# Query and key items of an indexer interleaved on one core, with value weights and first value tile moved into the stage

## What is computed

```python
xn = rms_norm(h, g)
cb, cc, ch, q, k, v, qi, ki, iw = split_projection(xn @ w_in, pos, q_g, k_g)
# qi: 8 indexer queries of 64 per token, rotated; ki: one indexer key of 64, rotated; iw: 8 head weights
dots = jnp.einsum('bthd,bsd->bths', qi, ki)
scores = jnp.einsum('bths,bth->bts', jax.nn.relu(dots), iw) * IDX_SCALE
# top-k of the scores chooses the keys of the attention; v are its values
```

## Time and profile before

| | before |
|---|---|
| median of 3 runs | 1865.98 us (1863.97 to 1866.81) |
| profiled execution | 1866.83 us, span 1865.0 us |
| TensorE busy, mean granted clock | 1721.9 us (92%), 0.955 |
| VectorE busy | 1116.0 us (60%) |
| ScalarE busy | 812.2 us (44%) |
| GpSimd busy | 732.3 us (39%) |

### The profile page before, as it was taken

One profiled execution on the slowest core, in us unless ns is written; L12 is line 12 of the kernel. 1 busy time (PEld: TensorE's weight loads), 2 busy tenths in 40 slices (PEclk: granted clock), 3 DMA queues, 4 the chain that ended last, 5 costly groups with the idle time before them and its releaser, 6 DMA issues.

```text
span 1865.0 us, 33809 instructions
## 1 busy us (share of the span) xinstructions
PE 1721.9 (92%) x13803; PEld 1193.3 (64%) x13803; DVE 1116.0 (60%) x1901; ACT 812.2 (44%) x1475; POOL 732.3 (39%) x705
## 2 busy tenths in 40 slices
PE   6899999996876889999979998999999999999998
PEld 3554444443444655444568644788888888898998
DVE  4965665787797865356645227878878887400000
ACT  5456487753643864332356315544434434210100
POOL 3131266887530110320032516666666666401200
PEclk9899999997986999999977999999999999999999
DMA  7031212122424110301244212112121122221211
GB/s 227 6 105 41 56 35 64 50 74 82 141 94 139 53 47 1 110 1 35 72 155 130 86 40 91 46 46 69 46 64 52 47 69 86 97 94 40 94 35 29
DMA packets 136548, 132.75 MB, mean 71 GB/s; under 512 B 15358, under 2 KB 109630, under 8 KB 136356
## 3 DMA queue, kind: packets, MB, share of 16 engines
q1 hardware_dynamic: 123850, 118.79, 20.5%
q10 hardware_dynamic: 12544, 11.80, 2.0%
HBM read 114.58 MB, written 15.98 MB: 70 GB/s over the span
## 4 chain that ended last, share of the span: by engine, by line
PE 72%; DVE 12%; ACT 6%; issue 3%; POOL 3%; DMA 2%; SPq 0%; ACTq 0%; DVEq 0%; POOLq 0%
PE PS L1533 22%; PE PS L937 5%; PE PS L938 5%; PE PS L939 5%; PE PS L1590 5%; PE PS L1591 5%; PE PS L1592 5%; ACT arena L1606 2%; ACT arena L1665 2%; PE PS L1088 2%; PE PS L1090 2%; PE PS L1089 2%; PE PS L1235 2%; PE PS L1247 1%; POOL arena L2917 1%
## 5 line engine op out<-in xcount | busy, mean ns | idle before, releaser
L1533 PE MATMUL PS<-arena 128*128 128x272 f16 (+1 forms) x3696 | 430.5, 280 | 5.9 <-issue 5.9
L1533 PEld LDWEIGHTS PS<-arena 128*128 128x128 f16 (+1 forms) x3696 | 362.6, 98 | 73.8 <-issue 6.1
L1606 ACT ACTIVATE arena<-PS 128x512 f16<-128x512 f32 (+13 forms) x380 | 190.1, 530 | 234.8 <-PE PS L939 85.2
L368 POOL TENSOR_TENSOR arena<-arena 128x512 bf16<-128x512 f32 (+2 forms) x152 | 166.6, 1132 | 241.8 <-ACT arena L359 241.5
L1606 ACT ACTIVATE arena<-arena 128x512 f16<-128x512 f32 (+5 forms) x214 | 136.1, 657 | 235.5 <-PE PS L1533 116.0
L937 PE MATMUL PS<-arena 128*128 128x512 f16 (+3 forms) x648 | 231.2, 366 | 2.3 <-DVE arena L2557 1.4
L938 PE MATMUL PS<-arena 128*128 128x512 f16 (+3 forms) x648 | 230.8, 365 | 0.0
L939 PE MATMUL PS<-arena 128*128 128x512 bf16 (+3 forms) x648 | 230.4, 364 | 0.0
L1590 PE MATMUL PS<-arena 128*128 128x256 f16 (+1 forms) x792 | 216.0, 273 | 1.4 <-POOL arena L915 1.0
L1592 PE MATMUL PS<-arena 128*128 128x256 bf16 (+1 forms) x792 | 215.9, 273 | 0.0
L1591 PE MATMUL PS<-arena 128*128 128x256 f16 (+1 forms) x792 | 215.9, 273 | 0.0
(11 more groups left out here) (350 smaller groups left out, 3712.5 us busy)
## 6 DMA issues: line engine op xcount, KB each, us to landing
arena<-w_gu SPq DMA_DIRECT2D x44, 512.0 KB, 4.8
arena<-w_down SPq DMA_DIRECT2D x8, 1408.0 KB, 7.7
arena<-w_in SPq DMA_DIRECT2D x8, 1024.0 KB, 5.5
arena<-w_kv_mem SPq DMA_DIRECT2D x8, 1024.0 KB, 5.3
arena<-cache_mem_k SPq DMA_DIRECT2D x32, 256.0 KB, 3.4
arena<-cache_mem_v ACTq DMA_DIRECT2D x28, 256.0 KB, 4.1
arena<-w_in SPq DMA_DIRECT2D x24, 256.0 KB, 3.9
arena<-x_prompt SPq DMA_DIRECT2D x9, 512.0 KB, 6.4
```

The lines of the kernel that those rows point to most:

```text
L368: x = e.tensor_tensor(w_lo[self.slot(n)][:, 4 * half + k, 0:width], wst[half][:, k, 0:width], w_hi[self.slot(n)][:, 4 * half + k, 0:width] ...
L1533: mm = e.matmul(PS[:, product_bank(f, i) + c, 0:TC], w[:, i, k], s[i][:, q, c, :], start=first, stop=last)
L1606: e.activation(out, in_, ACT.Copy, **kw).then_inc(sem(name), 1)
```

## The change

The items come in turns, query 0, then query j and key j - 1 for j = 1 to 8, then key 8, and all three loops run over items instead of steps. Slots of chunks are counted anew: the key weights get room of their own in the region `XM`, and the value weights take the slot that they leave. So the split of the value weights waits for nothing, and ScalarE does it in items 5 and 8, GpSimd in eight pieces behind the rotations of items 6 to 13. The first value tile (eight steps) is done by TensorE behind the projection of the last item and the transpose of query 8; the other 64 steps are spread over the 48 dots. SyncE stores the first seven keys before it loads three constants of the selection. Cut to its core:

```diff
-                if n >= 2:
-                    name, count = self.used(n - 2)
-                    e.wait_ge(sem(name), upto(name, count))
-                for half in range(2):
+                before = self.used(n - 2) if n >= 2 else None
+                if before:
+                    e.wait_ge(sem(before[0]), upto(*before))
+                for half in halves:
...
-                    lambda n: ("s2_mm", NT * (n + 1)) if n < 2 else ("v_mm", NT) if n == 2 else
-                    ("s4_mm", NT * (n - 2)) if n < 7 else ("s2_mm", NT * (n - 4)))
+                    lambda n: None if n == 0 else ("s2_mm", NI1) if n == 1 else ("v_mm", NT) if n == 2 else
+                    ("s4_mm", NT * (n - 2)) if n < 7 else ("s2_mm", NT * (n - 4)), odd=2,
+                    own={1: (view("XM", 0, [KT, D_IN - KIB], F16), view("XM", 2048, [KT, D_IN - KIB], BF16))})
...
-        ITEMS = [(c, j) for c in (A_QI, A_KI, A_Q, A_K) for j in range(NT)]
+        ITEMS = [(A_QI, 0)] + [it for j in range(1, NT) for it in ((A_QI, j), (A_KI, j - 1))] + [(A_KI, NT - 1)]
+        ITEMS += [(c, j) for c in (A_Q, A_K) for j in range(NT)]
...
         def values_upto(m):
-            return VSTEPS * max(0, m + 1) // ND
+            return KT + (VSTEPS - KT) * (m + 1) // ND if m >= -1 else 0
...
             A.load(e, 2)
+            store_roped(A_KI, range(NB - 1))
             e.wait_ge(sem("n1_lo"), NT)
...
-            store_roped(A_KI)
+            store_roped(A_KI, range(NB - 1, NT))
...
+            N1.pe_turn(e, 0, lambda j: h[0:rows(j), j, :])
+            for L in range(NI1 + 2):
+                if L < NI1:
+                    c, j = ITEMS[L]
+                    if c == A_QI:
+                        if j + 1 < NT:
+                            N1.pe_turn(e, j + 1, lambda j: h[0:rows(j), j, :])
+                        e.wait_ge(sem("n1_lo"), j + 1)
+                    if L >= 2:
+                        e.wait_ge(sem("s2_raw"), L - 1)
+                    project_item(L)
+                if L >= 2:
+                    turn_item(L - 2)
+                if L == NI1 - 1:
+                    e.wait_ge(sem("n1_lo"), NT)
+                    for k in range(KT):
+                        value_step(0, k)
...
+            N1.act_root(e, 1)
+            N1.act_hi(e, 0)
+            for L in range(NI1 + 2):
+                if L < NI1:
                     c, j = ITEMS[L]
+                    if c == A_QI and j + 2 < NT:
+                        N1.act_root(e, j + 2)
+                    if c == A_QI and j + 1 < NT:
+                        N1.act_hi(e, j + 1)
                     n, w = rows(j), A.chunks[c][1]
                     e.wait_ge(sem("s2_mm"), L + 1)
                     if L >= 3:
                         e.wait_ge(sem("s2_roped"), L - 2)
                     copy(raws[0][0:n, L % 3, 0:w], PS[0:n, L % 2, 0:w], "s2_raw")
-                    if j == 0:
-                        A.split_hi(e, c + 1)
-                if step >= 4:
-                    item_hi(step - 4)
+                    if L == 0:
+                        A.split_hi(e, A_KI)
+                    if L in (5, 8):
+                        A.split_hi(e, A_V, [int(L == 8)])
+                if L >= 2:
+                    item_hi(L - 2)
...
+            for j in range(3):
+                N1.dve_norm(e, j, lambda j: h[0:rows(j), j, :])
+                if j >= 1:
+                    N1.dve_lo(e, j - 1)
+            e.wait_ge(sem("turns_ld"), 32)
+            for L in range(NI1 + 2):
+                if L < NI1:
+                    c, j = ITEMS[L]
+                    if c == A_QI and j + 3 < NT:
+                        N1.dve_norm(e, j + 3, lambda j: h[0:rows(j), j, :])
+                    if c == A_QI and j + 2 < NT:
+                        N1.dve_lo(e, j + 2)
+                    project_item(L)
+                if L >= 2:
+                    item_lo(L - 2)
...
-            for n in range(3):
-                A.split_lo(e, n)
+            A.split_lo(e, A_QI)
+            A.split_lo(e, A_KI)
+            for half in range(2):
+                e.wait_ge(sem("wa_hi"), 2 * A_V + half + 1)
+                for k in range(4):
+                    e.wait_ge(sem("s2_roped"), 7 + 4 * half + k)
+                    x = e.tensor_tensor(A.low(A_V)[:, 4 * half + k, :], wst[half][:, k, :],
+                                        A.high(A_V)[:, 4 * half + k, :], ALU.subtract)
+                x.then_inc(sem("wa_lo"), 1)
```

More of the change, by code:

```diff
@@ L346, in load, with split_hi @@
                         c += w
-            def split_hi(self, e, n):
+            def split_hi(self, e, n, halves=(0, 1)):
                 if n >= len(self.chunks):
@@ L366, in split_lo @@
                     for k in range(4):
-                        x = e.tensor_tensor(w_lo[self.slot(n)][:, 4 * half + k, 0:width], wst[half][:, k, 0:width],
-                                            w_hi[self.slot(n)][:, 4 * half + k, 0:width], ALU.subtract)
+                        x = e.tensor_tensor(self.low(n)[:, 4 * half + k, :], wst[half][:, k, 0:width],
+                                            self.high(n)[:, 4 * half + k, :], ALU.subtract)
                     x.then_inc(self.s("lo"), 1)
@@ L694, in _, with store_roped @@
             const(pts[:, :], io["page_table"].rearrange("a b -> (a b)")[None, :])
-            def store_roped(c):
+            def store_roped(c, js=range(NT)):
                 for k in STORED:
-                    if ITEMS[k][0] == c:
+                    if ITEMS[k][0] == c and ITEMS[k][1] in js:
                         j = ITEMS[k][1]
@@ L994, in project_item, with value_step @@
                 mm.then_inc(sem("s2_mm"), 1)
[L996 to L1002, removed]
+            def value_step(j, k):
+                if k == 0 and j == 0:
+                    A.ready(e, A_V)
+                if k == 0 and j == 2:
+                    e.wait_ge(sem("st_ev"), 2)
+                if k == 0 and j >= 4:
+                    e.wait_ge(sem("v_ev"), j - 3)
+                out = PS[0:rows(j), 4 + j % 4, :]
+                wh, wl = A.high(A_V)[:, k, :], A.low(A_V)[:, k, :]
+                e.matmul(out, xa_hi[:, k, tcols(j)], wh, start=(k == 0), stop=False)
+                e.matmul(out, xa_lo[:, k, tcols(j)], wh, start=False, stop=False)
+                mm = e.matmul(out, xa_hi[:, k, tcols(j)], wl, start=False, stop=(k == KT - 1))
+                if k == KT - 1:
+                    mm.then_inc(sem("v_mm"), 1)
+            N1.pe_turn(e, 0, lambda j: h[0:rows(j), j, :])
[6 more added lines that the diff above has]
+                        e.wait_ge(sem("n1_lo"), j + 1)
                     if L >= 2:
@@ L1005, in _ @@
                     project_item(L)
-                if step >= 4:
-                    turn_item(step - 4)
+                if L >= 2:
[4 more added lines that the diff above has]
+                        value_step(0, k)
             e.wait_ge(sem("const"), 16 * CONSTS)
-            e.wait_ge(sem("n1_lo"), NT)
             for f in range(NC_T):
@@ L1020, in _ @@
             e.wait_ge(sem("s2_lo"), split_items(NI1))
[L1022 to L1033, removed]
-                mm = e.matmul(out, xa_hi[:, k, tcols(j)], wl, start=False, stop=(k == KT - 1))
-                if k == KT - 1:
-                    mm.then_inc(sem("v_mm"), 1)
             for m, (i, hh) in enumerate(DOTS):
@@ L1084, in _ @@
                 for k in range(KT):
-                    wh, wl = (w[c % 2][:, k, g * P:(g + 1) * P] for w in (w_hi, w_lo))
+                    wh, wl = (w[:, k, g * P:(g + 1) * P] for w in (A.high(c), A.low(c)))
                     xh, xl = xa_hi[:, k, t0:t0 + tn], xa_lo[:, k, t0:t0 + tn]
```

34 lines of the change are left out of this document (7 added, 27 removed).

## The result

The changed kernel is slower. Its median is 1877.17 us, and 1877.18 when it ran again, where the kernel before stood at 1866.0 and 1866.9 beside it.

A forecast was written before the change was run, and what follows sets the result against it. It took a chain of waits across VectorE, TensorE and ScalarE to set the new rounds, TensorE being full in the dots. Terms 1.4 + 0.5 - 2.6 + 0.45 + 0.5 + 5.1 + 1.7 = +7.0 gave 1873.0 us, range 1857 to 1879.

The forecast's parts named there:

- The round: Query-key rounds before the dots: 9.8 us each, a chain through VectorE, TensorE's transpose, ScalarE's copy and root.
- The clock in the rounds: Rounds before the dots: TensorE's gaps of some 2 us lower its clock, +0.5 us (0 to +3).
- The end of the stage: After the last norm: TensorE sets the pace, with a short wait for query 8's rotation; dots start at 108.8.
- Value tile 0: Ahead of the dots: as long as a query item, 5.2 us, taken out of the dots.
- The split of the second half: ScalarE's split of the value weights between a key item's copy and the next round's first copy: +1.6 us.
- GpSimd's pieces at 0: Eight value-weight pieces behind item rotations: no cost while VectorE waits for the root, up to 8.9 us otherwise.
- The start of the dots, -2.6 and +0.45: First dots: low clock goes, -2.6 us; ScalarE's copies of value tile 0 delay the third dot, +0.45.
- The wait at dot 14, +5.1 and +1.7, with 0.5 at dot 10: Dots: third value tile waits for GpSimd, TensorE stands 5.1 us; low clock +1.7; relu 8 behind the splits +0.5.
- Rival 1: Rounds before the dots: TensorE sets them at 7.4 us, result -8.1, 1857.9 us; chance 0.13.
- Rival 2: Dots: no wait at dot 14, result -0.3, 1865.7 us; chance 0.15.
- both together: TensorE sets the rounds and no wait comes at dot 14: -15.4, 1850.6 us; chance 0.05.

The follow-up runs named there:

- the second profile: The unaltered changed kernel run once more, with its own profiled execution of 1874.64 us; median 1877.18 us, ratio 1.0066 against the kernel before.
- the two cures: Changed kernel with GpSimd making value tile 0's low part before the conv weights' and VectorE's norm one tile later; 1857.24 us, ratio 0.9946.
- the third edit: Second half of the value weights split in item 7 instead of 8, added to GpSimd's order and VectorE's later norm; 1854.50 us, again 1855.00.
- norm lag: Changed kernel with VectorE's norm and low part of a token tile one turn later; 1862.95 us, ratio 0.9984.
- split at item 7: Changed kernel with ScalarE splitting the second half of the value weights in item 7 instead of item 8; 1883.21 us, ratio 1.0072.
- tile in the dots with the cures: Changed kernel with VectorE's later norm, the item 7 split and the first value tile among the dots, GpSimd's order unaltered; 1858.83 us, ratio 0.9957.
- the three cures: Changed kernel with GpSimd's new order, VectorE's later norm and the split in item 7; 1854.50 us, run again 1855.00 us, ratio 0.9930.
- without pacing: Changed kernel with GpSimd's eight value-weight pieces starting as soon as ScalarE has split a half; 1886.52 us, ratio 1.0105.

## Why the prediction was right, point by point

The sign, the place and both waits were right, and the way to the first of them nearly so; 1873.0 against 1877.2 is 4.2 too little. In profiled executions it is +10.3 at the last value step where the sum says +7.0. The dots took 78.30 us where the sum gives 78.9, so the missing 3.3 are made of +3.9 in the stage and -0.6 behind it.

- **The round.** Right in what it says of norm and root, since moving one lag brings the period to 7.4, and right in size where the clock stayed up: 9.8 predicted, 9.9 and 9.8 in the second profile. The link from VectorE back to ScalarE was the wrong one of two: not the key item's low part, transpose and copy (0.15 + 0.33 + 0.28), but the query item's low part, its transposes, and three copies more on ScalarE. That both give 9.8 is in part luck, and it is why taking the predicted link away saved next to nothing in the later rounds.
- **The clock in the rounds** was the term that was mis-sized. With gaps of 1.95 and 3.78 us ahead of the four transposes comes low clock (from 53.1 to 56.5, and from 73.6, still in the gap, to 80.4), and the norm's transposes and a part of the projection fall into it: L442 takes 1.92 at 54.66, where it takes 1.06 at 64.41. I put +0.5 for all rounds, because the round has slack on TensorE. But the projection and the transpose of the key item are behind that gap too, and ScalarE needs both ahead of the root. To the sixth turn the stage took 2.0 more than the sum without this term: 0.3 ahead of the first turn, 1.7 in the rounds. Of the 1.7 the second profile has 1.2 less (50.5 us for 51.7), which is the low clock; the other 0.5 is not shown to be clock. So the scatter of the term is larger than what I gave it.
- **The end of the stage.** I let the turn of query 8 wait only for its rotation. It waits for the low part of query 7 (the 1.90 at 103.88), which VectorE makes behind the rotation of query 8: +1.4 missed. This is the same kind of order as in the round, and I had written it out for the round only.
- **Value tile 0** was to run at the full clock. In the stretch behind the gap of 1.90 it did not (windows of one us each). It took 6.9 us (104.24 to 111.12) where 5.2 was counted, +1.7; what follows it up to the first dot took 2.1 where I had 2.7, -0.6:

```profile
105.00:106.00 1.00, 1.00 (x4) 0.41 (x3) 0.93 (x6) 0.00 (x0) 0.00 (x0) 0.50 0.14 32
...
107.00:108.00 1.00, 1.00 (x4) 0.40 (x3) 0.00 (x0) 0.00 (x0) 0.00 (x0) 0.64 0.08 16
```

- **The split of the second half** at +1.6: right. The longest round is the one that has it, 11.7 in both profiles, 1.8 over its neighbours of 9.9 and 9.8 in the second; 0.6 to 0.9 of it is removable by one item's shift. The first half cost nothing that shows.
- **GpSimd's pieces at 0**: right for the changed kernel, as they fall into VectorE's wait for the root. They cost up to 0.7 a round (8.1 for 7.4) as soon as this wait is taken away, and more when unpaced. The price of 0 was that of a cover, and the cover was the loss.
- **The start of the dots, -2.6 and +0.45**: right in kind. No low clock at 113.2, and the experiment that puts the tile back has it again. By that experiment it is 1.6 in the dots, for 2.15.
- **The wait at dot 14, +5.1 and +1.7, with 0.5 at dot 10**: right in place, releaser and size. ScalarE idle 4.81 (4 to 5 predicted), gaps of 4.48 and 0.42 on TensorE, low clock from 135 to 138.4. All of it together is 6.0 to 6.5 by the experiment, where I counted 7.3:

```profile
135.00:136.00 1.00, 0.42 (x2) 0.15 (x3) 0.37 (x1) 1.00 (x3) 0.89 (x1) 0.51 0.57 215
...
138.00:139.00 1.00, 1.00 (x5) 0.42 (x4) 0.39 (x1) 0.00 (x0) 0.00 (x0) 0.78 0.30 66
```

- **The rivals.** Rival 1 (TensorE sets the rounds) was priced at 15.1 with its clock term, and one lag on VectorE gave 14.2. Rival 2 was priced at 7.3, and one order on GpSimd gave 6.5. So the prices of the two waits held from the other side too. As times of their own the rivals were too low: both together were forecast at 1850.6, and the two cures gave 1857.2, with the third edit 1854.5 to 1855.0. They left out what the sum left out (the last round), and GpSimd's pieces, which cost something once VectorE has no wait to hide them.

## What to carry to other kernels

When loops on several engines are re-lagged, write one round down as a chain, engine by engine, and follow what each in-order engine has ahead of the instruction that the next one waits for, along every way that leads back and not only the first found; the sum of the links of the longest way, and not the largest load, is the period, and one place in one engine's order can be worth 14 us in five rounds. Do this for the last, odd round as well. Work moved out of one stage brings the next one's copies forward too, and these can reach a producer that was at the edge of being late: ask who was last to be just in time.

## What the runs showed of the hardware

One stretch comes in two lengths, in all kernels alike. From the last value step to the first conv product TensorE does the scores of the sample tokens, small float32 products. It took 16.0 us in the profiles of before, of the changed kernel and of seven of the experiments, and 21.9 to 22.5 us in four others (norm lag, both cures, split at item 7, and tile in the dots with the cures). The windows over it, of before, of the three cures run again, and of the kernel with the tile in the dots and the cures:

```profile
186.50:196.80 10.30, 9.46 (x32) 3.12 (x33) 4.33 (x12) 2.90 (x6) 0.00 (x0) 1.00 0.34 96
```

```profile
174.60:185.00 10.40, 9.49 (x33) 3.18 (x34) 4.39 (x12) 2.92 (x7) 0.00 (x0) 1.00 0.30 86
```

```profile
177.20:193.70 16.50, 15.64 (x32) 4.49 (x32) 4.30 (x12) 2.93 (x7) 0.00 (x0) 0.55 0.22 61
```

The same 32 or 33 products at a granted clock of 1.00 or of 0.55, for 10.4 or 16.5 us. The runs of one kernel lie in two groups about as far apart (norm lag: 1859 to 1864 and above 1870; without pacing: 1879 and 1886 to 1887), so I take this for their cause. That is not shown, as there is one trace of each kernel; the traced executions fit it (norm lag 1870.15 with the long form, without pacing 1879.00 with the short one). What decides it is open: the last gap of TensorE ahead of it is the same in both. A difference under some 6 us between two variants needs the windows of this stretch beside it, or many runs.

Short gaps of TensorE are not safe either. The gaps of 1.95 at 52.58 and 1.90 at 103.88 in the changed kernel were followed by 3.4 us at 0.50. But nothing followed gaps as long in the rounds of its second profile (1.95 at 51.38, 1.98 at 61.25) or ahead of the value tile in the kernel with three cures (1.90 at 86.77). The length of such a gap alone does not tell; the +0.5 of the prediction, from one gap of 2.09, allowed for too little of it.
